# A two-layer attention and expert trunk on one core: w_out and decay loaded in one go, two tiles of output begun ahead, low parts of the fox heads moved forward, retention gated from the bank

## Chip, cores and metric

The kernel runs on one core of a Trainium2 chip. The metric is the device time of one execution in microseconds (us); the median of three runs is quoted. Every number of the trace comes from one profiled execution.

## The reference, cut to what matters

```python
D_MODEL, SEQ, DEPTH = 1024, 512, 2
FOX_HEADS, FOX_HEAD_DIM, RET_HEADS, RET_HEAD_DIM = 8, 64, 4, 128
for layer in range(DEPTH):
    x = x + mixer(rmsnorm(x, norm_mix_w[layer]), w_in[layer], fox_forget_b[layer], w_out[layer])
    x = x + hierarchical_moe(rmsnorm(x, norm_ffn_w[layer]), ...)        # 32 experts, top 2 in one of 4 groups
return rmsnorm(x, norm_final_w)

def mixer(h, w_in, fox_forget_b, w_out):
    fq, fk, fv, ff, rq, rk, rv, rg = split(h @ w_in)
    fox = forgetting_attention(fq, fk, fv, cumsum(log_sigmoid(ff + b)))      # causal softmax, 8 heads of 64
    ret = retention(rotary(rq), rotary(rk), rv)          # (q k^T * decay) v, 4 heads of 128
    ret = head_rmsnorm(ret) * silu(rg)
    return concatenate([fox, ret]) @ w_out

def expert_block(xblk, e):
    return (silu(xblk @ w_expert_gate[e]) * (xblk @ w_expert_up[e])) @ w_expert_down[e]
```

All arrays are float32. One layer's 32 experts have 32 x 3 matrices of 2 MB, 201 MB in all.

## The kernel before

One large SBUF tensor, `area`, holds everything that changes place. Its first three slots of 12,288 columns (`EXPERT`) are the ring for expert weights; in attention the same space holds the normed input (`h_hi`, `h_lo` in slot 0), queries, keys, values, the retention's gate `rg` and its table of decay `dk` (slot 1), and the slabs of `w_in` and later `w_out` (slot 2). Behind the ring lie `mixed` (the eight 128-row chunks of attention output, four of fox heads, four of retention heads), the probabilities `prob`, and their transposes `probT`.

Products that need full precision are made of three: a float32 operand is split into a rounded half (`_hi`, by ScalarE) and the rest (`_lo`, by VectorE, or by GpSimd for weights), and TensorE adds hi*hi, hi*lo and lo*hi in a bank.

The order of work in attention is one list, `steps()`, which every engine walks in its own program and of which it carries out its own part; an engine never overtakes a step of its own. The list's names are: `S` (fox scores), `PT` (transposes of the probabilities, on TensorE, copied to `probT` by ScalarE), `PV` (value products), `gate` (three stages of the gate's sigmoid, ScalarE and VectorE in turn; a rule sets them behind the unit `rg` that they need), `RS` (retention scores, multiplied by decay on VectorE), `RV` (their value product), `RN` (the sum of squares over a head by a matmul with ones, then Ln, Exp and the product with the gated output), `mh` and `ml` (hi and lo of one chunk of `mixed`; ScalarE and VectorE), `ws` (hi of two of a `w_out` half's eight chunks on ScalarE; GpSimd makes the lo behind it, all eight in order), `wo` (t, half: output tile of 128 tokens x 512 columns, 8 chunks x 3 products), `begin` (the first chunks of a `wo`), `fT` and `lg` (the router's input transposed, and its logits). `banks()` gives each step one of the eight PSUM banks.

Loads are issued by SyncE in program order, each behind waits of its own. In late attention these are the two halves of `w_out`, the rest of decay, and then the first weights of experts 0 to 2, as the places become free. After the router's tables the expert loop begins: gate and up products, SiLU, down product, and the spread of the result to the tokens. From expert 3 on a load waits until the expert three before it has used the slot (`s_gh`, `s_gu`, `s_yf`).

## Time and profile before

| | |
|---|---|
| median of 3 runs | 1595.6 us (1594.26 to 1600.51) |
| profiled execution: time, span | 1595.73 us, 1593.2 us |
| TensorE busy in the span | 1483.2 us (93%) |
| VectorE busy | 816.8 us (51%) |
| ScalarE busy | 342.1 us (21%) |
| GpSimd busy | 270.0 us (17%) |
| DMA | 464.04 MB, 291 GB/s in the mean |

Shares are over the whole span. The busy time of TensorE counts an instruction from its start to its modelled end, and consecutive matmuls overlap, so that 93% doesn't say that it works at its peak. The stages differ: layer 0's attention runs to about 304 us and its experts to about 791 us; layer 1's attention follows to about 1089 us. PEclk is the clock granted to TensorE as a share of 2.4 GHz.

### The profile page before, as it was taken

The page shows a single profiled execution, that of the slowest core. Times are in us where ns is not written, and L with a number is a line of the kernel's source. Part 1 is how long each engine was busy: PE and PEld are TensorE (multiplying, and loading weights), DVE is VectorE, ACT ScalarE, POOL GpSimd, SP SyncE. Part 2 cuts the span into 40 slices and gives each one's busy share as a digit, 9 for nine tenths or more (in the row PEclk, how much of TensorE's full clock was granted, in tenths as well). Part 3 has the DMA queues.
Part 4 walks back from the last instruction along what each step waited for, and adds up shares of the span by engine and source line. Part 5 has one row for each costly group of instructions (what it writes and reads, how often), then busy time and mean ns, then how long its engine had stood idle before and what let it go on. Part 6 is the DMA issues. An engine that isn't in the chain of part 4 may idle for free.

```text
span 1593.2 us, 19190 instructions
## 1 busy us (share of the span) xinstructions
PE 1483.2 (93%) x7242; PEld 786.6 (49%) x7242; DVE 816.8 (51%) x1451; ACT 342.1 (21%) x654; POOL 270.0 (17%) x156
## 2 busy tenths in 40 slices
PE   5999998789999999999899999896999999998996
PEld 5877756643333333333378777485333333333332
DVE  4037756445555555454540686545355555545445
ACT  5335553100000000000152455520000000000002
POOL 3433313010000000000134331311000000000001
PEclk9999999889999999999999999997999999999998
DMA  4532144589999999999733320446999999999994
GB/s 146 133 89 71 41 178 172 198 359 420 419 419 419 419 419 419 420 419 420 285 106 94 87 71 14 178 185 246 419 419 420 418 419 420 418 419 419 420 420 197
DMA packets 124748, 464.04 MB, mean 291 GB/s; under 512 B 19026, under 2 KB 62162, under 8 KB 75504
## 3 DMA queue, kind: packets, MB, share of 16 engines
q1 hardware_dynamic: 117328, 450.18, 71.6%
q0 software_dynamic: 6272, 12.60, 2.1%
q8 instruction: 60, 0.98, 0.3%
q14 instruction: 32, 0.26, 0.0%
q10 hardware_dynamic: 1056, 0.00, 0.0%
HBM read 464.84 MB, written 6.29 MB: 296 GB/s over the span
## 4 chain that ended last, share of the span: by engine, by line
PE 63%; SPq 24%; DVE 5%; DMA 5%; issue 2%; ACT 1%; DVEq 0%; ACTq 0%
SPq L564 20%; PE bank L1610 15%; PE bank L1625 8%; PE bank L1463 5%; PE bank L1465 5%; PE bank L1464 5%; PE bank L1587 5%; SPq L574 4%; DMA area<-in_w_expert_up_dram 3%; PE bank L1529 2%; PE bank L1447 2%; PE bank L1448 2%; PE bank L1446 2%; PE bank L1530 2%; PE bank L1531 2%
## 5 line engine op out<-in xcount | busy, mean ns | idle before, releaser
L1610 PE MATMUL bank<-area 128*64 128x512 f32 x2048 | 468.3, 608 | 25.8 <-DMA area<-in_w_expert_up_dram 23.1
L1301 DVE TENSOR_TENSOR xres<-xres,bank 128x512 f32<-128x512 f32 x512 | 316.6, 682 | 1.8 <-PE bank L1587 1.8
L1610 PEld LDWEIGHTS bank<-area 128*64 128x64 f32 x2048 | 141.8, 139 | 318.7 <-issue 273.5
L1625 PE MATMUL bank<-area 128*64 128x512 f32 x1024 | 233.8, 598 | 6.9 <-DVE area L1308 2.1
L712 POOL DMA_INDIRECT area<-rows,gath x64 | 72.0, 1125 | 760.4 <-PE bank L1579 727.1
L1282 DVE TENSOR_TENSOR area<-area,bank 128x256 f32<-128x256 f32 x64 | 27.0, 421 | 337.0 <-ACT area L941 337.0
L687 POOL TENSOR_TENSOR w_lo<-area,w_hi 128x1024 fp32r<-128x1024 f32 x58 | 142.6, 2461 | 295.3 <-ACT w_hi L779 295.3
L941 ACT ACTIVATE area<-bank 128x256 f32<-128x256 f32 x64 | 24.6, 384 | 546.8 <-PE bank L1610 546.8
L1463 PE MATMUL bank<-h_hi,w_hi 128*128 128x512 f32 x336 | 134.7, 401 | 2.7 <-DVE h_lo L1138 2.7
L1625 PEld LDWEIGHTS bank<-area 128*64 128x64 f32 x1024 | 67.8, 136 | 131.7 <-issue 109.6
L1465 PE MATMUL bank<-h_hi,w_lo 128*128 128x512 f32 x336 | 131.1, 390 | 0.0
L1464 PE MATMUL bank<-h_lo,w_hi 128*128 128x512 f32 x336 | 131.0, 390 | 0.0
L1587 PE MATMUL bank<-y_hi,onehot 64*128 64x512 f32 x512 | 116.0, 447 | 9.0 <-DVE xres L1301 5.8
L950 ACT ACTIVATE y_hi<-bank,slot_w 128x512 fp32r<-128x512 f32 x64 | 44.0, 688 | 333.6 <-PE bank L1625 333.6
L1587 PEld LDWEIGHTS bank<-y_hi,onehot 64*128 64x128 f32 x512 | 48.5, 184 | 118.1 <-issue 106.6
L1587 PE MATMUL bank<-y_lo,onehot 64*128 64x512 f32 x512 | 102.7, 394 | 0.0
L1286 DVE SCALAR_TENSOR_TENSOR y_lo<-bank,slot_w,y_hi 128x512 fp32r<-128x512 f32 x64 | 48.1, 751 | 71.1 <-ACT y_hi L950 71.1
L779 ACT ACTIVATE w_hi<-area 128x1024 fp32r<-128x1024 f32 x58 | 61.1, 1057 | 68.5 <-PE bank L1448 39.3
L1463 PEld LDWEIGHTS bank<-h_hi,w_hi 128*128 128x128 f32 x336 | 63.0, 187 | 25.3 <-issue 9.5
L1465 PEld LDWEIGHTS bank<-h_hi,w_lo 128*128 128x128 f32 x336 | 63.1, 188 | 13.6
L1464 PEld LDWEIGHTS bank<-h_lo,w_hi 128*128 128x128 f32 x336 | 63.1, 188 | 12.0
L1159 DVE COPY area<-bank 128x512 f32<-128x512 f32 x8 | 5.5, 692 | 114.4 <-PE bank L1465 114.4
(172 smaller groups left out, 1667.4 us busy)
## 6 DMA issues: line engine op xcount, KB each, us to landing
area<-in_w_expert_up_dram SPq DMA_DIRECT2D x128, 1024.0 KB, 27.0
area<-in_w_expert_gate_dram SPq DMA_DIRECT2D x128, 1024.0 KB, 25.1
area<-in_w_expert_down_dram SPq DMA_DIRECT2D x64, 2048.0 KB, 29.2
area<-in_w_in_dram SPq DMA_DIRECT2D x58, 512.0 KB, 3.9
area<-in_w_out_dram SPq DMA_DIRECT2D x4, 2048.0 KB, 8.9
rows<-area POOLq DMA_DIRECT2D x8, 512.0 KB, 5.4
xres<-in_x_dram SPq DMA_DIRECT2D x4, 512.0 KB, 6.4
out_dram<-area SPq DMA_DIRECT2D x4, 512.0 KB, 3.4
```

Source lines behind the costliest of these rows:

```text
L564: sp.dma_start(wexp[slot][0][:, i, c0:c1, :].rearrange("p c n -> p (c n)"), weight[layer, bass.ds(e, 1), P * c0:P * c1, :] .rearrange("a ( ...
L574: sp.dma_start(wexp[slot][1].rearrange("p (b j) n -> p b (j n)", b=2), down_rows(layer, e)).then_inc(s_w[slot][2], 16)
L687: nc.gpsimd.tensor_tensor(w_lo[g % CUT][:, :, :], slab[g % RAW], w_hi[g % CUT][:, :, :].bitcast(F32), ALU.subtract).then_inc(s_wlo, 1)
L712: pool.indirect_dma_start(out=xg[e % 3], out_offset=None, in_=rows_dram, in_offset=bass.IndirectOffsetOnAxis(ap=gath[:, e:e + 1], axis=0), ...
L779: nc.scalar.activation(w_hi[g % CUT][:, :, :], slab[g % RAW], ACT.Copy).then_inc(s_whi, 1)
L1301: tt(xs, xs, bank[4 + i][:, :], ALU.add).then_inc(s_sa[i], 1)
L1463: mm(o[:, :], hi[:, c, :], h_hi[:, c, :], start=(c == 0), stop=False)
L1464: mm(o[:, :], hi[:, c, :], h_lo[:, c, :], start=False, stop=False)
L1465: last = mm(o[:, :], lo[:, c, :], h_hi[:, c, :], start=False, stop=(c == KC - 1))
L1587: yield mm(bank[4 + 2 * (t % 2) + half][:, :], onehot[parity][rows, P * t:P * (t + 1)], part[rows, :], start=(w_ == 0), stop=(w_ == 1))
L1610: last = mm(bank[1][SLOTS * half:SLOTS * (half + 1), :], xT[:, c % 4, c // 4, :], w[:, :, c, 256 * half:256 * (half + 1)], start=(c == 0), ...
L1625: last = mm(bank[3][SLOTS * half:SLOTS * (half + 1), :], hx[:, c % 2, c // 2, :], w[:, c, 512 * half:512 * (half + 1)], start=(c == 0), st ...
```

## The change

Seven things are done in each layer.

1. Decay is loaded whole (1 MB) where only its first quarter was, early in attention, and not in late attention any more. `probT[1]`, which lay on the late quarters' place, moves to the upper half of `mixed`.
2. Both halves of `w_out` and the up rows of expert 0 are loaded as soon as the last unit of `w_in` is done.
3. `wo_hi[0]` and `wo_hi[1]` change places. So expert 0's gate rows are loaded behind `wo` (3, 0) and expert 2's down rows at the end; expert 0's down rows are loaded when its gate rows were.
4. `mh` and `ml` of the first three fox chunks move ahead of retention; in the list 0 and 1 come right behind the last score slot and 2 behind `RS` (0, 2).
5. `ws` steps are spread: 0 and 1 before `RS` (1, 0), then one for each few steps.
6. The first six of eight chunks are begun for both halves of tiles 0 and 1 (4 x 18 products, in banks 1, 0, 2 and 3), where five were for tile 0 (2 x 15). What is begun is left out of `wo` later, so that the number of products stays.
7. VectorE multiplies the retention output in its bank by the gate in step `RV`; ScalarE's copy of it and VectorE's product in `RN` go. The bank is then freed by VectorE.

```diff
@@ steps
     last = [("PT", FH - 2), ("PT", FH - 1)]
-    out += [("RS", 0, 0), ("RS", 0, 1)] + [(*h, 0) for h in last] + [("PV", FP - 2, 3), ("RS", 0, 2)]
+    out += [("mh", 0), ("mh", 1), ("ml", 0), ("ml", 1)]
+    out += [("RS", 0, 0), ("RS", 0, 1)] + [(*h, 0) for h in last] + [("PV", FP - 2, 3), ("RS", 0, 2), ("mh", 2), ("ml", 2)]
     out += [(*h, 1) for h in last] + [("PV", FP - 1, 0)]
     out += [(*h, 2) for h in last] + [("RS", 0, 3), ("PV", FP - 1, 1)]
-    out += [(*h, 3) for h in last] + [("RS", 1, 0), ("PV", FP - 1, 2), ("RS", 1, 1), ("PV", FP - 1, 3)]
+    out += [(*h, 3) for h in last] + [("ws", 0), ("ws", 1), ("RS", 1, 0), ("PV", FP - 1, 2), ("RS", 1, 1), ("PV", FP - 1, 3)]
+    out += [("mh", 3), ("ws", 2)]
     out += [("RS", 1, 2), ("RS", 1, 3)]
-    leading = [[("mh", 0), ("ws", 0), ("ws", 1)], [("mh", 1), ("mh", 2), ("ws", 2), ("ws", 3)],
-               [("mh", 3), ("mh", 4), ("ws", 4), ("ws", 5)], [("mh", 5), ("ws", 6), ("ws", 7)]]
-    rest = [[], [("ml", 0)], [("ml", 1), ("ml", 2)], [("ml", 3), ("ml", 4)]]
-    for r in range(RH):
-        if r and r + 1 < RH:
-            out += [("RS", r + 1, j) for j in range(NT)]
-        out += rest[r] + [("RV", r)]
-        if r:
-            out += [("RN", r - 1)]
-        out += leading[r]
+    out += [("RV", 0), ("ws", 3)] + [("RS", 2, j) for j in range(NT)] + [("ml", 3)]
+    out += [("RV", 1), ("RN", 0), ("mh", 4), ("ws", 4)] + [("RS", 3, j) for j in range(NT)] + [("ml", 4)]
+    out += [("RV", 2), ("RN", 1), ("mh", 5), ("ws", 5), ("ml", 5)]
+    out += [("RV", 3), ("RN", 2), ("ws", 6), ("mh", 6), ("ml", 6), ("begin", 0, 0), ("RN", 3), ("ws", 7)]
+    out += [("begin", 0, 1), ("mh", 7), ("ml", 7), ("begin", 1, 0), ("begin", 1, 1)]
...
-    out += [("begin", 0, 0), ("ml", 5), ("RN", RH - 1), ("mh", 6), ("ml", 6), ("begin", 0, 1), ("mh", 7), ("ml", 7)]
@@ SyncE
-                    sp.dma_start(at(DK0, T), decay[:, 0:T]).then_inc(s_decay, 16)
+                    sp.dma_start(at(DK0, RH * T), decay).then_inc(s_decay, 16)
...
                 is_full(sp, UNITS[-1], layer)
-                load_w_out(0)
-
-                is_full(sp, ("O", FH // 2 - 1), layer)
-                sp.dma_start(at(DK0 + T, (RH - 1) * T), decay[:, T:]).then_inc(s_decay, 16)
-                load_w_out(1)
-
+                for half in range(2):
+                    load_w_out(half)
                 for half in range(2):
                     load_rows(layer, 0, 0, half, 1)
...
                 is_full(sp, ("wo", 3, 0), layer)
-                load_down(layer, 2, 2)
+                for half in range(2):
+                    load_rows(layer, 0, 0, half, 0)
                 for half in range(2):
                     load_rows(layer, 2, 2, half, 0)
...
-                for half in range(2):
-                    load_rows(layer, 0, 0, half, 0)
+                load_down(layer, 0, 0)
                 sp.wait_ge(s_gat[0], 16 * (layer * len(range(0, NE, 3)) + 1))
-                load_down(layer, 0, 0)
                 for half in range(2):
                     load_rows(layer, 2, 2, half, 1)
+                load_down(layer, 2, 2)
@@ ScalarE, RV
                         nc.scalar.activation(tmp[r % 2], bank[b][:, :], ACT.Square).then_inc(s_sq, 1)
-                        nc.scalar.activation(probT[0][:, T * (r % 2):T * (r % 2 + 1)], bank[b][:, :], ACT.Copy
-                                             ).then_inc(freed[b], 2)
@@ VectorE, RN and RV
                         y, m = probT[0][:, T * (r % 2):T * (r % 2 + 1)], mixed[:, RH + r, :]
-                        link(tt(y, y, rg[:, r, :], ALU.mult))
+                        is_taken(dve, ("RV", r), layer)
                         tt(m, m, y, ALU.mult).then_inc(s_ret, 1)
+                    elif kind == "RV":
...
+                        dve.wait_ge(s_sq, layer * RH + r + 1)
+                        tt(probT[0][:, T * (r % 2):T * (r % 2 + 1)], bank[b][:, :], rg[:, r, :], ALU.mult
+                           ).then_inc(freed[b], 2)
@@ TensorE
-                        split_at = KC - 3
-                        for c in range(split_at if s[:2] == ("wo", 0) else 0, split_at if kind == "begin" else KC):
+                        split_at = KC - 2
+                        for c in range(split_at if kind == "wo" and t < 2 else 0, split_at if kind == "begin" else KC):
```

The first place is VectorE's program around the last gates, behind the last fox scores. L1198 and L1191 are the third gate stage of head 2 and the first of head 3, L1227 the decay products of `RS` (0, 0) and (0, 1), L1194 the second gate stage of head 3. Before:

```order
L1217 TENSOR_SCALAR area<-area,rowsum 128x512
L1198 TENSOR_TENSOR area<-area 128x512
L1191 SCALAR_TENSOR_TENSOR area<-area 128x512
L1227 TENSOR_TENSOR area<-bank,area 128x512
L1227 TENSOR_TENSOR area<-bank,area 128x384
L1194 SCALAR_TENSOR_TENSOR area<-area 128x512
```

With the change (L1222 is `ml`, L1189, L1182, L1216 and L1185 are the lines just named, in the new file):

```order
L1208 TENSOR_SCALAR area<-area,rowsum 128x512
L1222 TENSOR_TENSOR mix_lo<-area,mix_hi 128x512 x2
L1189 TENSOR_TENSOR area<-area 128x512
L1182 SCALAR_TENSOR_TENSOR area<-area 128x512
L1216 TENSOR_TENSOR area<-bank,area 128x512
L1216 TENSOR_TENSOR area<-bank,area 128x384
L1185 SCALAR_TENSOR_TENSOR area<-area 128x512
```

Two low parts now stand ahead of both gate stages.

The second place is VectorE's program from the decay products of head 3 on. L1233 is `ml`, L1241 and L1242 are the two products of `RN`. Before:

```order
L1227 TENSOR_TENSOR area<-bank,area 128x128
L1233 TENSOR_TENSOR mix_lo<-area,mix_hi 128x512 x2
L1241 TENSOR_TENSOR area<-area 128x512
L1242 TENSOR_TENSOR area<-area 128x512
L1233 TENSOR_TENSOR mix_lo<-area,mix_hi 128x512 x2
```

With the change (L1240 is the product of `RV` from the bank, L1231 the one that is left in `RN`):

```order
L1216 TENSOR_TENSOR area<-bank,area 128x128
L1222 TENSOR_TENSOR mix_lo<-area,mix_hi 128x512
L1240 TENSOR_TENSOR area<-bank,area 128x512
L1231 TENSOR_TENSOR area<-area 128x512
L1222 TENSOR_TENSOR mix_lo<-area,mix_hi 128x512
```

One low part in place of two stands ahead of head 1's normalised product, and the product with the gate reads a bank.

The third place is ScalarE's program from the last fox output copy (L880) on. L904 and L905 are Square and Copy of `RV`, L894 is `mh`, L885 is `ws`, L912 and L913 are Ln and Exp of `RN`. Before:

```order
L880 ACTIVATE area<-bank 128x512
L904 ACTIVATE area<-bank 128x512
L905 ACTIVATE area<-bank 128x512
L894 ACTIVATE mix_hi<-area 128x512
L885 ACTIVATE wo_hi_60<-area 128x1024 x2
```

With the change (L878 is `ws`, L873 the fox output copy, L887 `mh`, L897 the Square):

```order
L878 ACTIVATE wo_hi_60<-area 128x1024 x2
L873 ACTIVATE area<-bank 128x512
L887 ACTIVATE mix_hi<-area 128x512
L878 ACTIVATE wo_hi_60<-area 128x1024
L897 ACTIVATE area<-bank 128x512
L878 ACTIVATE wo_hi_60<-area 128x1024
```

Three `ws` steps moved ahead of the first retention head, and the copy is gone.

## Rows read from the trace of the kernel before

**Rows 1.** Windows: stretch, its length, busy us of TensorE, weight loads, VectorE, ScalarE, GpSimd, clock, DMA share, GB/s.

```profile
290.00:320.00 30.00, 19.27 (x116) 16.86 (x114) 15.27 (x47) 3.24 (x7) 2.84 (x3) 0.83 0.64 245
...
400.00:760.00 360.00, 348.04 (x1760) 131.59 (x1760) 187.18 (x327) 27.35 (x51) 26.27 (x23) 1.00 1.01 419
```

**Rows 2.** Chain of waits: start us, us, what.

```profile
223.68 4.46 DMA area<-in_decay_dram
...
296.31 2.60 PE bank L1544 x24
...
1080.92 2.60 PE bank L1544 x24
```

**Rows 3.** Timeline, SyncE's queue: start us, us, engine, line, operation, [idle before <-releaser].

```profile
331.74 0.33 SPq L564 DMA_DIRECT2D area<-in_w_expert_gate_dram  x1
```

**Rows 4.** Timeline, TensorE and its weight loads, layer 0.

```profile
228.97 2.42 PE L1507 MATMUL bank<-area 128*128 128x512 f32 x8 [2.32 <-DVE area L1227]
...
249.85 0.29 PEld L1529 LDWEIGHTS bank<-wo_hi,mix_hi 128*128 128x128 f32 x1 [4.95 <-DVE mix_lo L1233]
...
303.87 0.39 PE L1530 MATMUL bank<-wo_lo,mix_hi 128*128 128x512 f32 x1
...
304.10 0.39 PE L1531 MATMUL bank<-wo_hi,mix_lo 128*128 128x512 f32 x1
```

**Rows 5.** Windows in layers 0 and 1, columns as in the first group.

```profile
248.50:255.00 6.50, 5.15 (x10) 3.44 (x11) 6.46 (x5) 3.82 (x6) 4.74 (x3) 0.50 0.00 0
...
1013.00:1016.00 3.00, 3.00 (x8) 1.93 (x7) 1.98 (x5) 0.00 (x0) 3.00 (x2) 0.50 1.08 409
```

**Rows 6.** Timeline, TensorE in layer 1.

```profile
1011.83 3.75 PE L1507 MATMUL bank<-area 128*128 128x512 f32 x8 [2.45 <-DVE area L1227]
```

**Rows 7.** Timeline around the last gates, layer 0: ScalarE, VectorE, TensorE.

```profile
212.59 0.44 ACT L874 ACTIVATE area<-bank 128x128 f32<-128x128 f32 x2
...
212.72 0.69 DVE L1191 SCALAR_TENSOR_TENSOR area<-area 128x512 f32<-128x512 f32 x1 [1.25 <-ACT area L848]
...
213.45 0.63 ACT L852 ACTIVATE area<-area 128x512 f32<-128x512 f32 x1 [0.42 <-DVE area L1191]
...
214.11 0.72 ACT L853 ACTIVATE area<-area,kst 128x512 f32<-128x512 f32 x1
...
215.08 0.68 DVE L1194 SCALAR_TENSOR_TENSOR area<-area 128x512 f32<-128x512 f32 x1
...
216.34 1.06 ACT L874 ACTIVATE area<-bank 128x512 f32<-128x512 f32 x2
...
216.97 1.03 PE L1491 MATMUL bank<-kst,area 128*128 128x128 f32 x6 [0.59 <-ACT area L874]
```

**Rows 8.** Timeline in retention, layer 0: ScalarE, GpSimd, VectorE.

```profile
227.65 0.63 ACT L894 ACTIVATE mix_hi<-area 128x512 fp32r<-128x512 f32 x1
...
228.17 2.00 ACT L885 ACTIVATE wo_hi<-area 128x1024 fp32r<-128x1024 f32 x2
...
229.31 4.67 POOL L697 TENSOR_TENSOR wo_lo<-area,wo_hi 128x1024 fp32r<-128x1024 f32 x2 [37.45 <-ACT wo_hi L885]
...
230.20 1.73 DVE L1227 TENSOR_TENSOR area<-bank,area 128x512 f32<-128x512 f32 x4 [0.29 <-PE bank L1507]
...
231.85 2.67 DVE L1233 TENSOR_TENSOR mix_lo<-area,mix_hi 128x512 fp32r<-128x512 f32 x1
...
234.08 0.59 ACT L905 ACTIVATE area<-bank 128x512 f32<-128x512 f32 x1
...
238.98 4.69 DVE L1233 TENSOR_TENSOR mix_lo<-area,mix_hi 128x512 fp32r<-128x512 f32 x2
...
241.00 0.63 ACT L913 ACTIVATE area<-area 128x512 f32<-128x512 f32 x1
```

**Rows 9.** Windows where the early decay load stands, layers 0 and 1.

```profile
46.00:48.00 2.00, 2.00 (x10) 1.65 (x10) 0.00 (x0) 1.05 (x2) 1.97 (x1) 1.00 0.03 11
...
788.00:792.00 4.00, 3.02 (x16) 0.72 (x10) 2.31 (x5) 1.78 (x3) 3.26 (x3) 1.00 0.00 0
```

More of the change, by code:

```diff
@@ L78 @@
 assert KC * T <= FH * T and KC * 512 <= KC * T
-assert CA0 + T <= EXPERT and PB3 + PLEN <= 3 * EXPERT
+assert FP * T + PLEN <= KC * T and CA0 + T <= EXPERT and PB3 + PLEN <= 3 * EXPERT
 assert WS0 + 2 * CUT * SLAB <= QT0 and WO0 + KC * D <= QT0
@@ L258, in banks @@
             b = 7
+        elif kind == "begin" and s[1]:
+            b = 2 + s[2]
         elif s not in where:
@@ L333, in trunk_kernel @@
         mix_hi, mix_lo = split("mix_hi", KT0, [KC, T]), split("mix_lo", MX0, [KC, T])
-        wo_hi = [split("wo_hi0", QT0, [KC, 512]), split("wo_hi1", HT0, [KC, 512])]
+        wo_hi = [split("wo_hi0", HT0, [KC, 512]), split("wo_hi1", QT0, [KC, 512])]
         wo_lo = [split(f"wo_lo{i}", WO0 + i * KC * 512, [KC, 512]) for i in range(2)]
@@ L339, in trunk_kernel @@
         prob = [at(start, PLEN) for start in (PB0, PB0 + PLEN, PB2, PB3)]
-        probT = [at(PT0, PLEN), at(DK0 + T, PLEN)]
+        probT = [at(PT0, PLEN), at(MX0 + FP * T, PLEN)]
         tmp = [at(TA0 + i * T, T) for i in range(2)]
@@ L439, in trunk_kernel @@
         s_sd = sem("decayed_scores_ready")
-        s_ro = sem("retention_out_ready")
         s_sq = sem("retention_square_ready")
@@ L590, in _ @@
                         sp.dma_start(at(CS0, 2 * T), rope).then_inc(s_rope, 16)
-                        sp.dma_start(at(DK0, T), decay[:, 0:T]).then_inc(s_decay, 16)
+                        sp.dma_start(at(DK0, RH * T), decay).then_inc(s_decay, 16)
                     if layer == 0 and n in (8, 10):
@@ L1222, in _ @@
                         if r == 0 and j == 0:
-                            dve.wait_ge(s_decay, 16 * (2 * layer + 1))
-                        if r == 1 and j == 0:
-                            dve.wait_ge(s_decay, 16 * (2 * layer + 2))
+                            dve.wait_ge(s_decay, 16 * (layer + 1))
                         is_full(dve, s, layer)
@@ L1240, in _ @@
                         y, m = probT[0][:, T * (r % 2):T * (r % 2 + 1)], mixed[:, RH + r, :]
-                        link(tt(y, y, rg[:, r, :], ALU.mult))
+                        is_taken(dve, ("RV", r), layer)
                         tt(m, m, y, ALU.mult).then_inc(s_ret, 1)
+                    elif kind == "RV":
+                        r = s[1]
+                        b, n = result(s, layer)
+                        is_full(dve, s, layer)
+                        dve.wait_ge(s_gate, RH * (layer + 1))
+                        if r >= 2:
+                            dve.wait_ge(s_ret, layer * RH + r - 1)
+                        dve.wait_ge(s_sq, layer * RH + r + 1)
+                        tt(probT[0][:, T * (r % 2):T * (r % 2 + 1)], bank[b][:, :], rg[:, r, :], ALU.mult
+                           ).then_inc(freed[b], 2)
                     elif kind == "wo":
@@ L1410, in _ @@
                     else:
-                        name, first = s, s[:2] != ("wo", 0)
+                        name, first = s, not (kind == "wo" and s[1] < 2)
                     if kind not in ("S", "fv", "rv"):
```

## The prediction

> **What bounds the kernel now.** I read the windows by stage first. Over the long expert stretch the 16 DMA engines are busy all the time at 419 GB/s, while late attention and routing, from 290 to 320 us, use them to 0.64 [rows 1]. So a layer has two parts. In its second part weights stream without a gap, and what is left to move then is a fixed amount; nothing but its start can be moved. The stream starts with the first load that waits for expert 0, which SyncE issues at 331.74 us [rows 3], and that is the end of a chain through attention, w_out and router. An attention stage that ends x us earlier should let the stream begin, and the layer end, x us earlier. In both layers. The reader is to see that TensorE's 93% says nothing here: what counts is where it waits ahead of the router.
>
> The chain of waits names the places: the late decay load at 223.68 us (4.46 us), and behind it the retention heads; the transposes and logits at 296.31 us are the same work in layer 1 at 1080.92 us, 784.61 later [rows 2]. The timeline gives the waits of TensorE in layer 0: 2.32 us for VectorE's decay products, which waited for that load, and 4.95 us (weight loads) for the low part of a mixed chunk, at 249.85 us; then it runs to 304.10 us, the last w_out product, product behind product 0.23 us apart, with no gap near these in length [rows 4]. The second wait costs more than itself: from 248.5 to 255.0 us the granted clock is 0.50 (1.2 GHz), and TensorE is busy 5.15 us in it [rows 5], which would be half as long at the full clock: 2.58 us lost. In layer 1 the decay wait is 2.45 us, and the scores behind it take 3.75 us where layer 0 had 2.42 [rows 4, 6], since from 1013 to 1016 us too the clock is 0.50 [rows 5]. The scores of layer 1 start 782.86 us after those of layer 0 (1011.83 less 228.97), the chain further on lags by 784.61: 1.75 us more for that fall [rows 2, 4, 6].
>
> **The change part by part.**
>
> *Decay and w_out early.* The decay wait goes: 2.32 us in layer 0; 2.45 + 1.75 = 4.20 in layer 1. The early load is 0.77 MB longer, 1.9 us at 419 GB/s. Cover: in layer 0 the engines are at 0.03 from 46 to 48 us, behind the slabs among which it stands, and in layer 1 at 0.00 from 788 to 792, where it is issued [rows 9]. So nothing; without cover 1.9 us a layer. SyncE queues w_out's second half and expert 0's up rows behind the first half; the first half is ahead of them in the queue. Nothing. The moved expert loads (gate 0 for down 2, down 0 for gate 0, down 2 for down 0) are 2 MB against 2 MB each time, and what comes later is needed by a later expert. Nothing.
>
> *Fox parts ahead of the gate.* This adds a wait. ScalarE ends the copies of head 4 and 5 at 212.59 + 0.44 = 213.03, then makes two high parts, 0.63 us each [rows 7, 8]. VectorE's two low parts and the third stage of gate 2 now stand ahead of gate 3's first stage, which began at 212.72 [rows 7]. It can begin with the first low part at 213.7, and three products of about 0.65 us bring it to 215.65. From that stage's start to the end of ScalarE's Ln were 214.11 + 0.72 - 212.72 = 2.11 us [rows 7]: 217.76, so the second stage starts at about 217.8 instead of 215.08, 2.7 us late. Behind it on ScalarE stands the copy of the first transposes of the last two heads (216.34), and for this copy TensorE waited already 0.59 us (216.97) [rows 7]. So 2.7 us are on the path, up to the first retention output. Bounds: 0, if TensorE has slack that I don't see; 3.3, if the third high part (0.63 us), which stands before the next copies, comes on top. I take 2.7.
>
> In layer 0 that is 0.38 us more than the decay wait it replaces. Against it, the ScalarE copy of 0.59 us [rows 8] is no more between a head's Square and its Ln; part of it was covered. I take the two as zero: TensorE comes to the first `begin` when it did, in layer 1 4.20 - 2.45 + 0.13 = 1.88 us sooner (what it lost against layer 0).
>
> *The gate's product from the bank, low parts rearranged.* The 4.95 us wait arose on VectorE: head 1's Exp was done by 241.63 (241.00 + 0.63), but two low parts in front of its products ran 4.69 us, from 238.98 on [rows 8]. The reason is in the rows: two low parts would take 1.4 us, but one that ran beside GpSimd's subtraction (229.31, 4.67 us for two) took 2.67, whereas four products with a bank as operand took 1.73 in all, beside it too [rows 8]. Now one low part stands there, and of the two products behind the Exp only one is left. I get the head's output at about 242.4, its high part at 243.1, its low part by 244, or by 246.5 if it meets a GpSimd subtraction. `begin` (0, 0) starts at about 242.7 and needs it for its sixth chunk, 15 products later: 246.1. So the wait of 4.95 us goes, and the slow clock behind it with its 2.58: 7.53 us a layer. Bounds for what is left of it: 0 and 0.4 us.
>
> Here a rule of the Trainium skill can be weighed. The row shows that the decay products kept their pace beside GpSimd [rows 8]. The page "SBUF — State Buffer" (section "SBUF: two separate sides") says that VectorE and GpSimd share a port pair as an exclusive lock, and that of such products only those with two SBUF inputs take part. By it the new product from the bank is never held; the trace agrees. Were it held as the low part was, by 2.0 us (2.67 against 0.69), once a layer on the path, the sum would be 4 us less.
>
> *More begun ahead.* 72 products before the last head's parts are needed instead of 30; the total stays. Behind `begin` (0, 1) stand now 36 more, 8 us, so that the last head's Ln, Exp, product, high and low part have 12 us of cover. What can come late is the fifth chunk of `begin` (0, 1), at 247.7 + 12 x 0.23 = 250.4: it needs the seventh `ws`. GpSimd's eight subtractions take 2.33 each, 18.7 us, from about 225; ScalarE reaches `ws` 6 at about 246 (2.00 us for two), GpSimd ends it at 249.3 [rows 8]. One us of margin; if it is short, TensorE waits 1 to 2 us.
>
> *Clock.* The fox wait is new idle time, some 3 us with its pauses. Idle of 2.32 us let the clock stand in layer 0, 2.45 us let it fall in layer 1 [rows 4, 6]. I count one fall in the two layers: 3.00 us of work at half clock are 1.5 us lost [rows 5].
>
> **Sum.** Layer 0 7.53; layer 1 7.53 + 1.88 = 9.41; less 1.5: 15.4 us. The profiled execution took 1595.73 us, its median neighbours 1595.6. I predict 1580.3 us.
>
> **The rivals.**
>
> *The fox wait does not reach the path, the clock stays* (0.10). Then 16.9 + 2 x 2.7 = 22.3: 1573.4 us. For it: TensorE has only 0.59 us of waiting there now. Against: that it waits for just this copy.
>
> *Half of it comes* (0.20). The clock falls after the fox wait in both layers, for a stretch as long as that of [rows 5] (2.6 us lost each), and `begin` (0, 1) waits 1.5 us for GpSimd: 16.9 - 5.2 - 3.0 = 8.7, 1587.0 us.
>
> *The stream hides it* (0.10). If the loads before the first experts set the start of the stream, TensorE's gain is waited away: 1595.7 us. For it: the same bytes are moved in less time. Against: the 0.64 of [rows 1] and that the loads in this stretch are released by the chain itself.
>
> *Slower* (0.08). The wait at the first `begin` only changes its name: if the low part of chunk 5 comes 5 us after TensorE wants it, the 7.5 us stay. With fox waits of 2 x 2.7 and clock falls of 2 x 2.6, less 2.32 and 4.20 for decay, that is 4.1 us more: 1599.8 us. It decides from 5 us of lateness on; I work out none.
>
> *Forecast* (0.52), its own range 1577 to 1584.
>
> **How the numbers follow.** Two measurements of this kernel can be told apart from about 0.5%, 8 us: faster is below 1587.6. Faster: 0.52 + 0.10 + two thirds of the 0.20 = 0.75. Same: the rest of it and the hidden case, 0.17. Slower 0.08. Range: from 1573, the case without a fox wait, to 1591, between the half gain and none; 0.18 at most are beyond.
>
> **What would show it.** VectorE no longer waits for decay; the first `RS` of head 2 starts at about 229.2 us in layer 0 (228.97 before). ScalarE's first copy for the last two fox heads starts at about 219.0, and TensorE idles before it. No wait over 1 us between the last head's RN and the last w_out product, the clock full there; last product near 296.6 us; first release of the stream near 324.2. In layer 1 the same with some 9 us. Wrong would be: a wait for `wo_lo` or `mix_lo` in a `begin` of some us; a DMA share under 1 after the stream's start; or expert 0 waiting for its gate rows.

## The result and the profile after

| | before | after |
|---|---|---|
| median (all runs) | 1595.29 us (1594.26 to 1600.51, 6 runs) | 1585.85 us (1582.52 to 1589.44, 6 runs) |
| profiled execution: time, span | 1595.73, 1593.2 us | 1589.44, 1587.4 us |

The ratio is 0.9934, 95% interval 0.9919 to 0.9950: faster, by 9.4 us in the median, where 15.4 were forecast, and below the 1587.6 us that the prediction set for it. The six times of after lie in two groups, 1582.5 to 1583.3 and 1588.4 to 1589.4, and the profile is of the upper one: it shows 6.3 us of gain, and part of the work below is to find what separates it from the forecast.

I read the windows first, as for before [rows 1].

```profile
290.00:320.00 30.00, 18.50 (x84) 16.06 (x83) 13.71 (x44) 3.24 (x7) 5.30 (x6) 0.64 0.60 228
400.00:760.00 360.00, 347.89 (x1758) 131.45 (x1756) 187.50 (x328) 26.80 (x50) 26.27 (x23) 1.00 1.01 419
```

The expert stretch is as full as it was, so the layer still has the two parts. SyncE's queue issues the first load that waits for expert 0 at 327.90 us, 3.84 earlier than before [rows 3]:

```profile
327.90 0.33 SPq L561 DMA_DIRECT2D area<-in_w_expert_gate_dram  x1
```

The further parts are read from TensorE's timeline, by the starts of a few products in each layer. Each number in this table is the start of one row.

| start on TensorE, us | before | after | after, second profile (e1_same) |
|---|---|---|---|
| first `RV` product, layer 0 | 224.32 | 228.31 | 228.16 |
| first `begin` product | 242.70 | 243.70 | 243.55 |
| last w_out product | 304.10 | 300.86 | 297.53 |
| expert 0's first product | 326.06 | 322.82 | 319.67 |
| layer 1's first product with `w_in` | 805.13 | 804.56 | 801.29 |
| first `RV` product, layer 1 | 1007.06 | 1010.36 | 1008.23 |
| first `begin` product | 1027.25 | 1025.74 | 1023.62 |
| last w_out product | 1088.68 | 1082.91 | 1079.16 |
| expert 0's first product | 1110.67 | 1104.90 | 1101.29 |

From expert 0 of layer 1 to the end of the span are 482.5 us in both kernels (1593.2 less 1110.67, 1587.4 less 1104.90): nothing is gained or lost there, and the whole difference is in the table.

**The fox wait.** Around the last gates VectorE, ScalarE and TensorE now show this, against [rows 7]; first the timeline:

```profile
213.59 1.29 DVE L1222 TENSOR_TENSOR mix_lo<-area,mix_hi 128x512 fp32r<-128x512 f32 x2 [2.69 <-ACT mix_hi L887]
...
216.13 0.63 ACT L845 ACTIVATE area<-area 128x512 f32<-128x512 f32 x1 [2.05 <-DVE area L1182]
216.75 0.70 PE L1506 MATMUL bank<-area 128*128 128x256 f32 x2 [0.99 <-DVE area L1216]
...
218.81 1.06 ACT L867 ACTIVATE area<-bank 128x512 f32<-128x512 f32 x2
219.44 1.39 PE L1490 MATMUL bank<-kst,area 128*128 128x128 f32 x6 [1.99 <-ACT area L867]
```

then the chain of waits at the same place (start, us, what):

```profile
214.81 0.68 DVE area L1189
215.49 0.61 DVE area L1182
216.13 0.64 ACT area L845
216.79 0.73 ACT area L846
217.54 0.70 DVE area L1185
218.47 0.34 issue
218.81 0.59 ACT area L867
219.44 1.39 PE bank L1490 x6
```

This is the step that the prediction worked out, at nearly its times: two low parts on VectorE, then the gate's stages in turn, the second at 217.54 (217.8 forecast), the copy of the transposes at 218.81 (219.0 forecast), and TensorE idle for it. TensorE waits 0.99 + 1.99 us where it waited 0.59: 2.4 us. The clock falls behind the wait (granted clock in the stretch, next-to-next-to-last column):

```profile
219.00:224.00 5.00, 4.56 (x18) 2.26 (x20) 1.74 (x4) 3.16 (x8) 0.00 (x0) 0.66 1.05 389
```

0.66 in the mean over 5 us is 1.7 us of full clock lost. 2.4 + 1.7 = 4.1, and the first `RV` product is 3.99 us later than before. The clock falls at this wait in both layers of all seven profiles that have the wait (after, e1_same, e3, e5, e6, e7, e8), and in none of the five without it.

**Retention.** The decay wait is gone; VectorE's decay products for head 1 wait for TensorE, and the scores of head 2 stand right behind the first `RV`, at 230.47 [rows 4]:

```profile
225.94 0.69 DVE L1216 TENSOR_TENSOR area<-bank,area 128x512 f32<-128x512 f32 x1 [1.74 <-PE bank L1506]
...
226.42 9.32 POOL L690 TENSOR_TENSOR wo_lo<-area,wo_hi 128x1024 fp32r<-128x1024 f32 x4 [34.55 <-ACT wo_hi L878]
...
230.47 2.32 PE L1506 MATMUL bank<-area 128*128 128x512 f32 x8
231.40 0.69 DVE L1240 TENSOR_TENSOR area<-bank,area 128x512 f32<-128x512 f32 x1 [2.42 <-ACT area L897]
...
233.60 2.70 DVE L1222 TENSOR_TENSOR mix_lo<-area,mix_hi 128x512 fp32r<-128x512 f32 x1
```

GpSimd works from 226.42 to 235.74. In this time VectorE's new product from the bank takes 0.69 us and the low part, both of whose inputs lie in SBUF, 2.70. The Trainium skill says in "SBUF — State Buffer", section "SBUF: two separate sides", that of such products only those with two SBUF inputs can be held by the lock that VectorE shares with GpSimd; these rows agree. From the first `RV` to the first `begin` are 15.39 us, where there were 18.38.

**The last stretch before the router.** No `mix_lo` or `wo_lo` wait is left in a `begin`: the 4.95 us of [rows 4] are gone, and the clock at that place is full. Why they are gone can be read from the rows of before. First TensorE's timeline, which has nine products from 242.70 to 244.94:

```profile
242.70 0.79 PE L1529 MATMUL bank<-wo_hi,mix_hi 128*128 128x512 f32 x1
...
244.94 0.39 PE L1531 MATMUL bank<-wo_hi,mix_lo 128*128 128x512 f32 x1
249.85 0.79 PE L1529 MATMUL bank<-wo_hi,mix_hi 128*128 128x512 f32 x1 [4.53 <-DVE mix_lo L1233]
```

then VectorE's:

```profile
244.31 2.74 DVE L1242 TENSOR_TENSOR area<-area 128x512 f32<-128x512 f32 x1
...
246.97 3.44 DVE L1233 TENSOR_TENSOR mix_lo<-area,mix_hi 128x512 fp32r<-128x512 f32 x2
```

Three products make a chunk, so that TensorE waited at the fourth chunk, a fox chunk. Its low part is the first of the two from 246.97 on. In VectorE's list it stood behind two other low parts (from 238.98 on, [rows 8]) and head 1's two products, of which the second took 2.74 us beside GpSimd. In after the same low part is the one at 233.60 above, done 9.9 us before TensorE's tenth product, at 246.18.

But TensorE's clock now falls further on, in the router's transposes and logits, with no idle time before it:

```profile
286.68 1.04 PE L1536 MATMUL bank<-kst,xres 128*128 128x128 f32 x8
287.55 1.87 PE L1543 MATMUL bank<-rtw,area 128*128 128x36 f32 x16
289.26 0.63 PE L1536 MATMUL bank<-kst,xres 128*128 128x128 f32 x4
289.73 3.54 PE L1543 MATMUL bank<-rtw,area 128*128 128x36 f32 x24
293.08 0.77 PE L1528 MATMUL bank<-wo_hi,mix_hi 128*128 128x512 f32 x1
293.65 0.63 PE L1529 MATMUL bank<-wo_lo,mix_hi 128*128 128x512 f32 x1
...
298.34 0.40 PE L1528 MATMUL bank<-wo_hi,mix_hi 128*128 128x512 f32 x1
...
300.86 0.39 PE L1530 MATMUL bank<-wo_hi,mix_lo 128*128 128x512 f32 x1
```

The reader is to see the last group of 24 logits, 3.54 us (2.77 in the second profile, below), and behind it large products 0.43 us apart instead of 0.23, up to 298.34. The windows of both layers say the same:

```profile
291.00:299.00 8.00, 8.00 (x29) 6.75 (x29) 1.30 (x2) 0.00 (x0) 0.72 (x1) 0.57 0.98 381
...
1073.00:1080.00 7.00, 7.00 (x25) 6.03 (x25) 1.30 (x2) 0.00 (x0) 0.72 (x1) 0.51 1.01 389
```

TensorE is busy all the time, at a mean clock of 0.57 and 0.51: 3.4 us lost in each layer. The second profile of the same kernel (the third column, next section) has no such stretch in layer 0.

### The profile page after: what moved, and what is told of

It is laid out like the page before. It is cut to its first block, busy times and chain, and to the rows that moved or that the text cites. A ratio compares the mean times of both kernels' runs of the same rounds, so it can differ in the third digit from the quotient of the medians.

```text
span 1587.4 us, 19196 instructions
## 1 busy us (share of the span) xinstructions
PE 1484.9 (94%) x7242; PEld 788.8 (50%) x7242; DVE 800.5 (50%) x1451; ACT 339.2 (21%) x646; POOL 267.8 (17%) x156
## 4 chain that ended last, share of the span: by engine, by line
PE 65%; SPq 24%; DMA 4%; DVE 3%; issue 2%; ACT 1%; DVEq 0%; ACTq 0%
SPq L561 20%; PE bank L1609 16%; PE bank L1624 8%; PE bank L1462 5%; PE bank L1464 5%; PE bank L1463 5%; PE bank L1586 5%; SPq L571 4%; DMA area<-in_w_expert_up_dram 3%; PE bank L1528 2%; PE bank L1529 2%; PE bank L1530 2%; PE bank L1447 2%; PE bank L1445 2%; PE bank L1446 2%
```

## The experiments

All times are medians. Each set has its own runs of before on its chip. Theory at the outset: the fox parts cost the path about 4 us a layer, the fall in the router's stretch another 3; rival: what is missing lies elsewhere (the begins, the loads, the stream).

### The first set: before 1598.35 us (1594.85 to 1600.73, 11 runs)

**e1_same.** The kernel after, unchanged.

> The changed kernel again, for the spread of its times. Its six runs so far fall in two groups, 1582.5 to 1583.3 us and 1588.4 to 1589.4. Clock theory: the upper group (to which the profiled execution belongs) has in each layer a fall of TensorE's clock to 0.50 in the stretch of router transposes and logits, 3.2 us a layer; so about half the runs lie near 1582.7 and half near 1589, and a profile of the lower group shows 24.5 us, not 27.7, from the long logits group to the slot weights' matmuls. Rival (the stream of weights starts or ends at another phase): the same two groups, but with the stream's start at the same time in both.

Measured: 1584.88 us (1580.92 to 1586.47, 6 runs), ratio 0.9914 (0.9897 to 0.9930); profile 1585.69, span 1583.1. On TensorE's timeline of this profile:

```profile
289.57 2.77 PE L1543 MATMUL bank<-rtw,area 128*128 128x36 f32 x24
292.17 0.48 PE L1528 MATMUL bank<-wo_hi,mix_hi 128*128 128x512 f32 x1
292.49 0.40 PE L1529 MATMUL bank<-wo_lo,mix_hi 128*128 128x512 f32 x1
...
297.53 0.39 PE L1530 MATMUL bank<-wo_hi,mix_lo 128*128 128x512 f32 x1
```

and the window that stood at 0.57 in the first profile:

```profile
291.00:299.00 8.00, 7.06 (x38) 5.75 (x38) 1.99 (x3) 0.21 (x1) 0.73 (x1) 1.00 1.00 386
```

The same instructions, at the same places to 0.2 us, run at the full clock. From the first `begin` to the last w_out product are 53.98 us, against 57.16 in the first profile and 61.40 before: 3.2 us for the fall alone, and 7.42 us of gain without it, where 7.53 was forecast. So one program runs this stretch with and without the fall. (In layer 1 of this profile a shorter one is left, 55.54 us.)

**e2_fox_late.** The fox parts are set back into the gaps of the last two fox heads.

```diff
-    out += [("mh", 0), ("mh", 1), ("ml", 0), ("ml", 1)]
-    out += [("RS", 0, 0), ("RS", 0, 1)] + [(*h, 0) for h in last] + [("PV", FP - 2, 3), ("RS", 0, 2), ("mh", 2), ("ml", 2)]
-    out += [(*h, 1) for h in last] + [("PV", FP - 1, 0)]
-    out += [(*h, 2) for h in last] + [("RS", 0, 3), ("PV", FP - 1, 1)]
-    out += [(*h, 3) for h in last] + [("ws", 0), ("ws", 1), ("RS", 1, 0), ("PV", FP - 1, 2), ("RS", 1, 1), ("PV", FP - 1, 3)]
+    out += [("RS", 0, 0), ("RS", 0, 1)] + [(*h, 0) for h in last] + [("PV", FP - 2, 3), ("RS", 0, 2)]
+    out += [(*h, 1) for h in last] + [("mh", 0), ("PV", FP - 1, 0)]
+    out += [(*h, 2) for h in last] + [("mh", 1), ("RS", 0, 3), ("ml", 0), ("PV", FP - 1, 1)]
+    out += [(*h, 3) for h in last] + [("mh", 2), ("ws", 0), ("ws", 1), ("RS", 1, 0), ("ml", 1), ("PV", FP - 1, 2), ("RS", 1, 1), ("ml", 2), ("PV", FP - 1, 3)]
```

> The changed kernel with the high and low parts of the first three fox chunks set one by one behind the probabilities' copies of the last two heads, where ScalarE and VectorE are idle, and no longer ahead of the last gate. My theory: the wait of 2.0 us for the copy, at 219.4 us, and the slow clock behind it go; the first retention product starts at 224.3 us as in the kernel before and not at 228.3, 4.0 us a layer, so the time falls by 7 to 8 us against the changed kernel, if the clock does not fall elsewhere. Rival (the fox wait is not on the path, since something behind it is just as late, such as GpSimd's low parts of w_out): under 2 us.

Measured: 1577.26 us (1574.90 to 1580.00, 4 runs), ratio 0.9866 (0.9849 to 0.9884): 7.6 us under e1_same. TensorE's timeline:

```profile
217.00 1.03 PE L1489 MATMUL bank<-kst,area 128*128 128x128 f32 x6 [0.60 <-ACT area L866]
...
224.36 2.32 PE L1512 MATMUL bank<-area 128*128 128x512 f32 x8
```

The wait is back at 0.60 us, the clock stays, and the first `RV` starts at 224.36, 0.04 us behind before's, and 201.99 us into layer 1 (999.88 less 797.89; before 201.93, e1_same 206.94). The fox placement is the whole delay ahead of retention.

**e3_router_broken.** The first 18 of the 24 products of the last output tile's second half are done in the middle of the router's transposes and logits, between ("lg", 1, 1) and ("fT", 3, 0); the other six stay behind them.

```diff
-            ("fT", 2, 0), ("fT", 2, 1), ("lg", 1, 0), ("lg", 1, 1), ("fT", 3, 0), ("lg", 2, 0), ("lg", 2, 1),
+            ("fT", 2, 0), ("fT", 2, 1), ("lg", 1, 0), ("lg", 1, 1), ("begin", 3, 1), ("fT", 3, 0), ("lg", 2, 0), ("lg", 2, 1),
...
-                        for c in range(split_at if kind == "wo" and t < 2 else 0, split_at if kind == "begin" else KC):
+                        for c in range(split_at if kind == "wo" and (t < 2 or s[1:] == (3, 1)) else 0, split_at if kind == "begin" else KC):
```

> The changed kernel with the first 18 products of the last output tile half (3, 1) set between the router's transposes and logits, so that the 9.5 us of small matmuls fall into two pieces. Clock theory: the clock stays at 1.00 there; the upper group of times is gone, and the runs lie at 1582 to 1583.5 us, 3.3 us below the changed kernel's median. Rival (the two groups come from elsewhere): two groups as before, median unchanged.

Measured: 1582.16 us (1581.64 to 1584.37, 4 runs), ratio 0.9906 (0.9889 to 0.9924); its profile shows no fall in the router's stretch in either layer, and 54.02 us from the first `begin` to the last product. The median is 2.7 us under e1_same, the slowest run 2.1; the intervals overlap, so that the trace shows no fall there and the times don't prove its price. Nor does the trace prove the cause: the profile of e5_loads_before, below, has no fall there in either layer either (53.99 and 53.93 us), with the stretch unbroken. (The stretch of small matmuls is 6.4 us long in the first profile, 286.68 to 293.08, not 9.5 as expected above.)

**e4_both.** Both edits.

> The two edits together. If both theories hold: 1582.7 less 7 to 8, 1575 to 1576 us, in one group. If the fox wait is not on the path: 1582. If the clock falls again because the phase moved: a group some 6 us higher.

Measured: 1575.38 us (1573.84 to 1577.07, 4 runs), ratio 0.9858 (0.9841 to 0.9876), span 1574.2. The last w_out product starts at 294.00 us in layer 0, 10.1 us before that of before, and at 1068.70 in layer 1, 20.0 before. It is the fastest version of all, at the time expected, and its interval ends below the ones of e1_same and of before; against e2_fox_late it isn't told apart.

### The second set: before 1597.98 us (1594.88 to 1601.26, 12 runs)

**e5_loads_before.** After, with decay and w_out loaded as before, in two parts each.

```diff
-                    sp.dma_start(at(DK0, RH * T), decay).then_inc(s_decay, 16)
+                    sp.dma_start(at(DK0, T), decay[:, 0:T]).then_inc(s_decay, 16)
...
-                for half in range(2):
-                    load_w_out(half)
+                load_w_out(0)
+
+                is_full(sp, ("O", FH // 2 - 1), layer)
+                sp.dma_start(at(DK0 + T, (RH - 1) * T), decay[:, T:]).then_inc(s_decay, 16)
+                load_w_out(1)
...
-                            dve.wait_ge(s_decay, 16 * (layer + 1))
+                            dve.wait_ge(s_decay, 16 * (2 * layer + 1))
+                        if r == 1 and j == 0:
+                            dve.wait_ge(s_decay, 16 * (2 * layer + 2))
```

> The changed kernel with the loads of decay and w_out as before: a quarter of decay early, and behind the last fox output first the rest of decay, then w_out's second half and expert 0's up rows. My theory: the decay wait returns, though the fox parts are where the change put them: the load is issued at about 227.7 us, lands 4.5 us later, VectorE's decay products start at 232.2 and not at 225.9, and TensorE's next scores at 232.9 and not at 230.5: 2.4 us a layer and a fall of the clock in at least one, 5 to 8 us slower than the changed kernel. Rival (the fox wait has taken the place of the decay wait, so that the early load is worth nothing): no difference.

Measured: 1589.98 us (1589.90 to 1597.78, 7 runs), ratio 0.9965 (0.9945 to 0.9985). The decay wait is back, on VectorE and then on TensorE:

```profile
233.49 1.68 DVE L1221 TENSOR_TENSOR area<-bank,area 128x512 f32<-128x512 f32 x4 [8.59 <-DMA area<-in_decay_dram]
```

```profile
234.24 2.42 PE L1511 MATMUL bank<-area 128*128 128x512 f32 x8 [2.37 <-DVE area L1221]
```

From `RV` to `begin` are 18.02 us against 15.39 in layer 0, 2.6 us where 2.4 was expected, and 19.76 against 15.38 in layer 1, where the clock falls with the wait. By the ratios (0.9965; 0.9934 and 0.9914 for after) it is 5 to 8 us slower than after, as expected. The load follows the chain, so that it comes late whatever is gained ahead of it.

**e6_gate_in_rn.** After, with the gate's product in `RN` and ScalarE's copy as before.

```diff
+                        nc.scalar.activation(probT[0][:, T * (r % 2):T * (r % 2 + 1)], bank[b][:, :], ACT.Copy
+                                             ).then_inc(freed[b], 2)
...
-                        is_taken(dve, ("RV", r), layer)
+                        link(tt(y, y, rg[:, r, :], ALU.mult))
...
-                        tt(probT[0][:, T * (r % 2):T * (r % 2 + 1)], bank[b][:, :], rg[:, r, :], ALU.mult
-                           ).then_inc(freed[b], 2)
```

> The changed kernel with retention's gate as before: ScalarE copies the bank, VectorE multiplies by the gate behind the Exp. My theory: what took the 4.95 us wait away is mostly that the low parts of fox chunks no longer stand in front of head 1's products; head 1's low part ended at 244.9 us and was wanted at 247.2, so the second product (0.7 us, up to 2.7 beside GpSimd) costs 0 to 1 us a layer: 0 to 2 us slower than the changed kernel. Rival (the product from the bank is what removed the wait): the wait returns, 5 to 7.5 us a layer, 10 to 15 us slower.

Measured: 1588.99 us (1586.97 to 1590.67, 6 runs), ratio 0.9936 (0.9920 to 0.9952), the same as that of the first comparison of after. From `RV` to `begin` 15.79 us, 0.40 more than after; VectorE's two products stand behind each Exp again, and no `begin` waits for a low part. The bank product is worth some 0.4 us a layer, which the times alone don't tell from nothing; the 4.95 us went without it.

**e7_begins_before.** After, with five chunks begun for tile 0 alone.

```diff
-    out += [("begin", 0, 1), ("mh", 7), ("ml", 7), ("begin", 1, 0), ("begin", 1, 1)]
+    out += [("begin", 0, 1), ("mh", 7), ("ml", 7)]
...
-                        split_at = KC - 2
+                        split_at = KC - 3
...
```

> The changed kernel with the begun products as before: five chunks of both halves of tile 0. My theory: it costs about what the last head's parts come late. They were ready at 254.6 us in the changed kernel, and would be 0.7 earlier; TensorE would want them at 252.8: 1.2 us a layer, 2 to 3 us slower in all, with the clock at 1.00. Rival (the further products begun are the main gain, since without them the clock falls too): 3 to 4 us a layer, 6 to 8 us slower.

Measured: 1588.54 us (1582.34 to 1596.18, 6 runs), ratio 0.9924 (0.9904 to 0.9943). TensorE waits once in each layer for the last low part:

```profile
255.61 0.50 PE L1528 MATMUL bank<-wo_hi,mix_hi 128*128 128x512 f32 x1 [1.00 <-DVE mix_lo L1222]
```

From `begin` to the last product are 58.52 us against 57.16, both with the router's fall: 1.4 us a layer for the longer begins, and not the 4.95. The median alone, with times from 1582 to 1596 us, isn't told apart from after's.

**e8_only_fox.** Before, with only the fox parts moved ahead of the gates.

```diff
-    out += [("RS", 0, 0), ("RS", 0, 1)] + [(*h, 0) for h in last] + [("PV", FP - 2, 3), ("RS", 0, 2)]
+    out += [("mh", 0), ("mh", 1), ("ml", 0), ("ml", 1)]
+    out += [("RS", 0, 0), ("RS", 0, 1)] + [(*h, 0) for h in last] + [("PV", FP - 2, 3), ("RS", 0, 2), ("mh", 2), ("ml", 2)]
...
-    leading = [[("mh", 0), ("ws", 0), ("ws", 1)], [("mh", 1), ("mh", 2), ("ws", 2), ("ws", 3)],
+    leading = [[("ws", 0), ("ws", 1)], [("ws", 2), ("ws", 3)],
...
-    rest = [[], [("ml", 0)], [("ml", 1), ("ml", 2)], [("ml", 3), ("ml", 4)]]
+    rest = [[], [], [], [("ml", 3), ("ml", 4)]]
```

> The kernel before with only the fox parts moved ahead of the last gate. My theory: the first retention product is 4 us late, the late decay load with it, and the next scores start at 233 us and not at 229; in return VectorE has no low parts in front of head 1's products and the wait of 4.95 us falls to 2 to 3. Taken together within 3 us of the kernel before, on either side. Rival (the fox parts alone are the gain): 5 us or more faster than before. Rival (they only cost): 8 us slower.

Measured: 1608.88 us (1606.65 to 1611.23, 6 runs), ratio 1.0066 (1.0049 to 1.0084): slower. On TensorE's timeline:

```profile
219.71 1.39 PE L1492 MATMUL bank<-kst,area 128*128 128x128 f32 x6 [1.99 <-ACT area L875]
...
233.25 4.07 PE L1508 MATMUL bank<-area 128*128 128x512 f32 x8 [2.30 <-DVE area L1228]
...
252.74 0.50 PE L1530 MATMUL bank<-wo_hi,mix_hi 128*128 128x512 f32 x1 [0.77 <-DVE mix_lo L1234]
...
261.08 0.75 PE L1530 MATMUL bank<-wo_hi,mix_hi 128*128 128x512 f32 x1 [2.29 <-DVE mix_lo L1234]
```

The fox wait is there, the decay wait is there behind it (with products at the slow clock, 4.07 us for eight), and the low parts are still late, by less. With the first three low parts out of VectorE's way the fourth is ready in time: twelve products run before the wait at 252.74, which is at the fifth chunk. Alone, this part of the change costs 11 us, and my theory, within 3 us of before, falls.

### The third set: before 1597.10 us (1594.41 to 1600.41, 17 runs)

**e9_only_loads.** Before, with only decay and w_out loaded early; `probT[1]` takes the free half of `mixed`. The edit is the reverse of e5_loads_before's.

> The kernel before with only the loads changed: decay whole in its early place, w_out's halves one behind the other, the second half of the last fox heads' transposes moved to the free upper half of mixed. The order of steps is that of before. Theory: the decay wait (2.32 us in layer 0, 4.20 with its clock fall in layer 1) is on the path and nothing else stood behind it, so that the first retention output comes 2.3 us sooner and both experts' starts by about as much; about 6.5 us faster than before, ratio 0.996. Rival: the wait for the low part of a mixed chunk (4.95 us) takes over what the decay wait leaves, since its end is set by VectorE's and GpSimd's queues; then that wait grows to about 7.2 us, the last w_out product stays at 304 us, and the time is that of before within 2 us.

Measured: 1590.66 us (1589.07 to 1591.89, 6 runs), ratio 0.9953 (0.9940 to 0.9966): 6.4 us faster. TensorE's timeline:

```profile
245.83 0.50 PE L1524 MATMUL bank<-wo_hi,mix_hi 128*128 128x512 f32 x1 [1.83 <-DVE mix_lo L1228]
...
248.61 0.79 PE L1524 MATMUL bank<-wo_hi,mix_hi 128*128 128x512 f32 x1 [1.82 <-DVE mix_lo L1228]
```

The wait at the low parts did not grow by what decay gave, as the rival had it: it is 3.65 us in two pieces. From `RV` to the last product the gain is 2.3 us in layer 0 (77.51 against 79.78) and 4.3 in layer 1 (77.37 against 81.62).

**e10_before_router.** Before, with products of the last output tile's second half in the middle of the router's stretch, as in e3_router_broken. Since this kernel begins five chunks and not six, they are 15 (3.4 us), not 24 as the text below says.

> The kernel before, with the 24 products of the last output tile's second half begun in the middle of the router's transposes and logits instead of behind them; nothing else is changed. Theory: the fall of TensorE's clock in the stretch of small transposes and logits, which some executions show and others do not, is what spreads the times of before over some 6 us; with 5 us of large products in the middle of that stretch it does not fall. Then the times are those of before's quicker executions, about 1594 to 1596 us, with a spread of 2 to 3 us, and the median is 2 to 3 us under the one of before on this chip. Rival: the fall has nothing to do with the spread of before; then the spread stays at 6 us and the median at that of before.

Measured: 1596.63 us (1592.98 to 1599.27, 12 runs), ratio 0.9992 (0.9983 to 1.0002): no change, and the spread is 6.3 us as before's 6.0. My theory on the spread of before falls: fifteen products there change neither the spread nor the median, and the profiles of before and of this run both have the clock at 1.00 in the stretch. Its profile has a stretch at the lower clock at 229 to 233 us, which that of before has not (20.04 us from `RV` to `begin` against 18.38).

## Why the prediction was partly right

The time came out 5.5 us over the forecast in the median (1585.85 against 1580.3): inside the whole range, 1573 to 1591, outside the forecast's own, 1577 to 1584, and nearer to the rival *half of it comes* (1587.0). Against the profile of after the miss is 9.1 us; at expert 0's first product in layer 1 it is 9.7, and this can be placed term by term.

- *What bounds a layer: right.* The stream moves with the chain, 482.5 us from expert 0 on in both kernels.
- *Decay wait, 2.32 and 4.20 us: right.* From `RV` to `begin` TensorE gained 2.99 and 4.81 (18.38 to 15.39, 20.19 to 15.38). e5_loads_before puts 2.63 of it on the loads, e6_gate_in_rn 0.40 on the bank product; in layer 1, e5 and e6 make 4.38 and 0.41; alone the loads gave 6.4 us (e9_only_loads) where the two terms are 6.5. (The early load is 0.79 MB longer, not 0.77; nothing hangs on it.)
- *Fox wait, 2.7 us: right in its mechanism, its place and nearly its size (2.4), but the term was mis-sized by its clock.* The step "I count one fall in the two layers", 1.5 us in all, failed: 1.7 us were lost in each layer, so that the first `RV` came 3.99 and 3.87 us late (layer 1: 205.80 us into the layer against 201.93). In layer 1 of e1_same it cost more (206.94). And since the list around it could be set otherwise for nothing (e2_fox_late), this was the costliest single loss of the change, 7.6 us in the time. Whether ScalarE's high parts or VectorE's low parts weigh more in it was not tried.
- *The 4.95 us wait with its clock, 7.53 a layer: right without the router's fall (7.42, e1_same), 4.24 and 4.26 in the profile of after.* Its cause was named in part wrongly. The prediction took head 1's low part, the sixth chunk, for what `begin` waits for, and gave the credit to one low part fewer and one product fewer in front of it. The rows of before above show the wait at the fourth chunk, a fox chunk, whose low part came behind two other low parts and behind head 1's products; what took the wait away is that the fox low parts moved forward. e6_gate_in_rn shows that the product counts for little (0.3 us of this stretch), and e7_begins_before that the longer begins hold 1.4 us. e8_only_fox moves only the first three: the wait at the fourth chunk is gone, but later ones come up, and the stretch is 1.0 us shorter than before in layer 0 (60.37 against 61.40) and 1.8 longer in layer 1 (63.28 against 61.43), with a fall of the clock more. So the new places of the other low parts and of `ws` count too (GpSimd begins its subtractions at 226.42, 2.9 us sooner than in [rows 8]); how much each gives was not tried by itself. The sixth chunk's low part was done at 244.85 in after and wanted at 247.54 (244 and 246.1 forecast), so that reading did no harm to the sum.
- *"The clock full there": wrong, and the largest miss.* The router's stretch lost 3.2 us in each layer of this execution (57.16 and 57.17 us from `begin` to the last product, 53.98 without).
- *"ends x us earlier, in both layers": not quite.* Of 3.24 us gained at expert 0 of layer 0 only 0.57 arrive at layer 1's first product with `w_in`. Of the 2.7 that are missing 1.6 to 1.7 us are a fall at the last expert, in the windows below; the other 1.0 is lost in the stream itself, and its cause stays open. Measured against before, layer 1 gives back 1.3 to 3.1 us of expert 0's lead in the six profiles with such a fall, 0.2 to 0.8 in four without, and 2.7 in one more without (e6_gate_in_rn), which I can't explain.

The windows from 776 to 780 us, of after:

```profile
776.00:780.00 4.00, 4.00 (x14) 1.28 (x14) 2.14 (x4) 0.00 (x0) 0.00 (x0) 0.57 0.96 349
```

and of before, with TensorE's clock at 1.00 in place of 0.57:

```profile
776.00:780.00 4.00, 3.21 (x16) 1.36 (x18) 4.00 (x8) 0.00 (x0) 0.00 (x0) 1.00 0.94 378
```

Together: 6.6 (the stretch: 7.53 less 4.24 and less 4.26; 6.4 of it the router's falls) + 0.4 (fox, beyond what was counted, net of what retention gave more) + 2.7 (between the layers) = 9.7 us, the forecast's 15.44 less the 5.77 that expert 0 of layer 1 shows.

The rivals: a fox wait that doesn't reach the path is refuted by e2_fox_late, a stream that hides all by the first load of the stream, 3.84 us earlier, a wait that only changes its name by the timeline. *Half of it comes* named the right kind of loss, clock falls, but put 5.2 us of them behind the fox wait (3.4 found) and 3.0 on a GpSimd wait that isn't there. Why the clock falls in the router's stretch in some executions is not settled. That it is this stretch is what the traces show. Large products in its middle go with no fall in both profiles of the changed kernel that have them (e3_router_broken, e4_both); but e5_loads_before, e9_only_loads and before have none either without them, and two profiles of a thing that comes and goes don't prove it. The two groups of after's times, 6 us apart, would fit two router falls of 3.2 us, but the times of e1_same, the same kernel, lie between as well, and no profile of a time in the lower group exists to show it.

## What to carry to other kernels

Low-priority work that is moved forward must not stand between two engines that hand a short chain to and fro: here two short operations on each of the two engines ahead of it cost 2.4 us of wait and a clock fall on top, and the same work a few steps later in the list cost nothing. A load issued behind a semaphore of the chain that needs it stays late whatever is gained ahead of it; load it whole where the engines are idle. When a wait behind which the clock falls is taken away, look through the stretches behind it in several executions before its clock is counted as won.

## What the runs showed of the hardware

TensorE's granted clock fell from 1.00 to its lower level (0.5, 1.2 GHz) in a stretch in which TensorE had no idle time, only 128 x 128 transposes and 36-column logits in a row (52 instructions from 286.68 us on), and the large products behind them ran 0.43 us apart instead of 0.23 until it rose again: 3.2 us lost, in both layers of the first profile, not in layer 0 of the second, with the same program. The Trainium skill ("TensorE: Matmul & The Clock Gate", section "Part 4: PE-mode transpose") says that transposes don't count as busy time in the same way; that would fit the place, but layer 0 of e1_same and both layers of e5_loads_before have the same transposes at the full clock, and whether they or the logits weigh was not tried.

Idle time ahead of a fall: after 2.32 us the clock stood [rows 4] and after 2.45 it fell [rows 6], but in after it fell with 1.99 us and 0.99 us shortly before, in both layers. At the decay wait of layer 0 it fell after 2.30 us in e8_only_fox and stood after 2.37 in e5_loads_before, so that the length of one idle time alone doesn't decide. A fall in a stretch without idle time cost about 1.6 us (e1_same, layer 1) or 3.2 (after). And unchanged kernels spread by 6 us from one execution to the next (before: 1594.41 to 1600.41 in 17 runs), which bounds what a median of three can tell here.
